# High and low activations side by side in one 512-column operand, and that form of matmul in 23 more steps

## The reference, cut to what matters

```python
u = jnp.einsum('bsd,de->bse', xn, w_in[l])
q, k, v, xr, gr, ga, gb = jnp.split(u, splits, axis=-1)
ya = chunked_band_attention(q, k, v, rel_table[l]) @ w_attn_out[l]
...
yb = (hr * jax.nn.gelu(gr)) @ w_rnn_out[l]
gates = jax.nn.sigmoid(jnp.concatenate([ga, gb], axis=-1) + b_merge[l])
g_a, g_b = jnp.split(gates, 2, axis=-1)
h = h + (g_a * ya + g_b * yb) @ w_o[l]
hn = rmsnorm(h, norm_ffn_g[l])
gu = hn @ w_ffn_in[l]
g, up = jnp.split(gu, 2, axis=-1)
h = h + (jax.nn.silu(g) * up) @ w_ffn_out[l]
```

## Time and profile before

| what | value |
|---|---|
| median of three runs | 1126.95 us |
| the profiled execution, its own time | 1127.41 us |
| its span in the trace | 1125.7 us |
| TensorE busy / weight loads busy | 1113.4 us / 1038.7 us |
| VectorE, ScalarE, GpSimd busy | 765.1, 589.9, 218.2 us |
| granted TensorE clock, mean | 0.997 of 2.4 GHz |
| HBM traffic | 166 GB/s over the span |

### The profile page before, as it was taken

One profiled execution on the slowest core, in us unless ns is written; L12 is line 12 of the kernel. 1 busy time (PEld: TensorE's weight loads), 2 busy tenths in 40 slices (PEclk: granted clock), 3 DMA queues, 4 the chain that ended last, 5 costly groups with the idle time before them and its releaser, 6 DMA issues.

```text
span 1125.7 us, 19980 instructions
## 1 busy us (share of the span) xinstructions
PE 1113.4 (99%) x7954; PEld 1038.7 (92%) x7954; DVE 765.1 (68%) x943; ACT 589.9 (52%) x791; POOL 218.2 (19%) x216
## 2 busy tenths in 40 slices
PE   8999999999999999999999999999999999999997
PEld 8999999999888889999999988888899999888887
DVE  6656984666877754599886777764467657876443
ACT  6546557545655543665664556643354445665332
POOL 2996002302000000167844010000030002000000
PEclk9999999999999999999999999999999999999999
DMA  9674442655655555446410356555545444656541
GB/s 299 204 236 150 150 132 96 225 185 169 206 187 186 186 188 190 146 148 188 152 39 2 112 161 197 193 196 186 187 150 188 151 144 148 200 189 215 189 149 38
DMA packets 154994, 187.31 MB, mean 166 GB/s; under 512 B 6544, under 2 KB 143920, under 8 KB 154928
## 3 DMA queue, kind: packets, MB, share of 16 engines
q1 hardware_dynamic: 151360, 184.06, 50.4%
q10 hardware_dynamic: 3568, 2.31, 0.7%
HBM read 185.29 MB, written 1.07 MB: 166 GB/s over the span
## 4 chain that ended last, share of the span: by engine, by line
PE 87%; POOL 5%; DVE 5%; issue 1%; ACT 1%; DMA 0%; DVEq 0%; POOLq 0%; ACTq 0%
PE PS L445 18%; PE PS L493 12%; PE PS L386 10%; PE PS L387 9%; PE PS L388 9%; PE PS L447 9%; PE PS L495 6%; POOL XN L911 2%; DVE WL L382 2%; POOL TAP L909 2%; POOL XN L906 1%; PE PS L453 1%; PE PS L452 1%; PE PS L454 1%; PE PS L2013 1%; PE PS L2026 1%
## 5 line engine op out<-in xcount | busy, mean ns | idle before, releaser
L382 DVE TENSOR_TENSOR WL<-RAW,WH 128x2048 fp32r<-128x2048 f32 x170 | 399.1, 2349 | 213.0 <-ACT WH L373 212.9
L373 ACT ACTIVATE WH<-RAW 128x2048 fp32r<-128x2048 f32 x170 | 325.0, 1912 | 219.1 <-PE PS L495 121.1
L445 PE MATMUL PS<-XHL,WH 128*128 128x512 f32 x864 | 300.9, 395 | 0.0
L386 PE MATMUL PS<-XHL,WH 128*128 128x256 f32 x832 | 240.3, 289 | 3.0 <-DVE WL L333 1.8
L447 PE MATMUL PS<-XHL,WL 128*128 128x256 f32 x864 | 239.6, 277 | 0.0
L387 PE MATMUL PS<-XHL,WH 128*128 128x256 f32 x832 | 236.0, 284 | 0.0
L388 PE MATMUL PS<-XHL,WL 128*128 128x256 f32 x832 | 236.0, 284 | 0.0
L493 PE MATMUL PS<-HHL,WH 128*128 (+1 forms) x592 | 205.4, 394 | 0.0
L445 PEld LDWEIGHTS PS<-XHL,WH 128*128 128x128 f32 x864 | 162.1, 188 | 37.5
L386 PEld LDWEIGHTS PS<-XHL,WH 128*128 128x128 f32 x832 | 160.2, 193 | 6.4 <-issue 2.8
L495 PE MATMUL PS<-HHL,WL 128*128 (+1 forms) x592 | 164.0, 277 | 0.0
(11 more groups left out here) (310 smaller groups left out, 1669.4 us busy)
## 6 DMA issues: line engine op xcount, KB each, us to landing
RAW<-in_mlp_w_up SPq DMA_DIRECT2D x32, 1024.0 KB, 5.4
RAW<-in_mlp_w_down SPq DMA_DIRECT2D x32, 1024.0 KB, 5.0
RAW<-in_w_in SPq DMA_DIRECT2D x25, 1024.0 KB, 5.2
RAW<-in_w_ffn_in_pairs SPq DMA_DIRECT2D x22, 1024.0 KB, 5.1
RAW<-in_dn_w_in SPq DMA_DIRECT2D x16, 1024.0 KB, 5.9
RAW<-in_mb_w_in SPq DMA_DIRECT2D x12, 1024.0 KB, 5.2
RAW<-in_w_ffn_out SPq DMA_DIRECT2D x11, 1024.0 KB, 4.9
RAW<-in_w_attn_out SPq DMA_DIRECT2D x4, 1024.0 KB, 5.8
```

The source lines that it names most:

```text
L373: act.activation(WH[:, k], RAW[:, k], ACT.Copy).then_inc(hi_done, 1)
L382: dve.tensor_tensor(WL[:, k], RAW[:, k], WH[:, k].bitcast(F32), ALU.subtract).then_inc(lo_done, 1)
L386: pe.matmul(out, wh, xh, start=start, stop=False, skip_group_check=True)
L445: pe.matmul(out.rearrange("p (e t) -> p e t", e=2), h[:, k, part], XHL[:, :, k], start=(k == 0), stop=False, skip_group_check=True)
```

## The change

It does three things. (1) XHL, OH/OL, HHL and DOH/DOL are laid out with the high and low run of one block side by side ([8, 2, 256]), so the 512-column operand is one run of 512 numbers; this touches every wide matmul of the kernel. (2) The wide form is used in gab 4 to 7, ao, ro 0 to 2, wo, do and mo: 23 steps. Ro 3 stays narrow and only takes its banks from the table. (3) A table PAIRS gives the PSUM banks of these steps, and the halves are added by new work: ScalarE's `low_to` and VectorE's `add_to` in gab, ao and ro 0 to 2, a second addition to H on VectorE in wo, do and mo.

```diff
-    XHL = sb("XHL", [P, 2, KB, TOK], F32R, 80)
-    XH, XL = XHL[:, 0], XHL[:, 1]
+    XHL = sb("XHL", [P, KB, 2, TOK], F32R, 80)
+    XH, XL = XHL[:, :, 0], XHL[:, :, 1]
...
-    HHL = sb("HHL", [P, 2, 32, TOK], F32R, Z + 0)
-    HH, HL = HHL[:, 0], HHL[:, 1]
+    HHL = sb("HHL", [P, 32, 2, TOK], F32R, Z + 0)
+    HH, HL = HHL[:, :, 0], HHL[:, :, 1]
...
+        PAIRS = {"qk": (4, 6, 2, 4, 6, 2, 4, 6), "gab": (None, None, None, None, 3, 5, 0, 3), "ao": (5, 0, 2, 4),
+                 "ro": (6, 0, 4, 2), "wo": (6, 4, 2, 6), "do": (6, 4, 2, 6), "mo": (5, 2, 0, 6)}
...
-                pe.matmul(out.rearrange("p (e t) -> p e t", e=2), h[:, k, part], XHL[:, :, k], start=(k == 0), stop=False,
+                if not halves_:
+                    mm = product(pe, out[:, 0:TOK], h[:, k, part], l[:, k, part], both[:, k, 0], both[:, k, 1], k == 0, k == KB - 1)
+                    continue
+                pe.matmul(out, h[:, k, part], both[:, k].rearrange("p e t -> p (e t)"), start=(k == 0), stop=False,
                           skip_group_check=True)
...
+        def low_to(act, st, out):
+
+            act.wait_ge(mm_done, st.count())
+            act.activation(out, wide_sides(st)[1], ACT.Copy).then_inc(s_.part_out, 1)
+
+        def add_to(dve, st, out, n):
+
+            dve.wait_ge(s_.part_out, n)
+            return dve.tensor_tensor(out, out, wide_sides(st)[0], ALU.add)
...
                 merge_gate(2 * st.j - 8)
-                merge_gate(2 * st.j - 7)
+                if st.j < 7:
+                    merge_gate(2 * st.j - 7)
+                act.wait_ge(s_.scanned, 8)
+                low_to(act, st, GAB[:, 2 * st.j:2 * st.j + 2])
+            merge_gate(7)
...
-                read_out(st, GAB[:, 2 * st.j:2 * st.j + 2])
+                blk = slice(2 * st.j, 2 * st.j + 2)
+                ch(add_to(dve, st, GAB[:, blk], part_no("gab") + st.j - 3))
+                ch.wait(dve)
+                dve.tensor_tensor(GAB[:, blk], GAB[:, blk], by_rows(2), ALU.mult).then_inc(freed[st.slot], 1)
...
-                    dve.tensor_tensor(hb, hb, bank(st), ALU.add).then_inc(freed[st.slot], 1)
+                    ch(dve.tensor_tensor(hb, hb, wide_sides(st)[1], ALU.add))
+                    ch.wait(dve)
+                    dve.tensor_tensor(hb, hb, wide_sides(st)[0], ALU.add).then_inc(freed[st.slot], 1)
...
-            steps(pe, seg["ao"], lambda st: multiply(pe, st, OH, OL))
-            steps(pe, seg["ro"], lambda st: multiply(pe, st, XH, XL, (s_.y_done, 0) if st.j == 0 else None))
-            steps(pe, seg["wo"], lambda st: multiply(pe, st, OH, OL, (s_.ml_done, 0) if st.j == 0 else None))
+            steps(pe, seg["ao"], lambda st: multiply_wide(pe, st, both=OHL))
+            steps(pe, seg["ro"], lambda st: multiply_wide(pe, st, (s_.y_done, 0) if st.j == 0 else None, halves_=st.j < 3))
+            steps(pe, seg["wo"], lambda st: multiply_wide(pe, st, (s_.ml_done, 0) if st.j == 0 else None, both=OHL))
```

More of the change, by code:

```diff
@@ L267, in build @@
           amf_out yf_out ty_out zg_done vn0 vn0_out s_done s_out w_done w_out vn1 vn1_out o_done o_out osq osum ostat osd
[L268 removed]
+          orows gated uq_zero yy oo low_out outg part_out low_rows low_added hi_piece lo_piece sp_ready""".split()
         s = {n: sem(n) for n in names}
@@ L430, in wide_sides, with multiply_wide @@
             return both[:, :, 0], both[:, :, 1]
-        def multiply_wide(pe, st, pieces=None, between=None):
+        def multiply_wide(pe, st, pieces=None, between=None, both=XHL, beside=None, halves_=True):
             pe.wait_ge(lo_done, st.count())
@@ L438, in multiply_wide @@
             for n, (b, k) in enumerate(order_of(pieces)):
+                if n == 4 and beside:
+                    beside()
                 if n == KB and between:
@@ L444, in multiply_wide @@
                 part = slice(b * P, b * P + P)
-                pe.matmul(out.rearrange("p (e t) -> p e t", e=2), h[:, k, part], XHL[:, :, k], start=(k == 0), stop=False,
+                if not halves_:
+                    mm = product(pe, out[:, 0:TOK], h[:, k, part], l[:, k, part], both[:, k, 0], both[:, k, 1], k == 0, k == KB - 1)
+                    continue
+                pe.matmul(out, h[:, k, part], both[:, k].rearrange("p e t -> p (e t)"), start=(k == 0), stop=False,
                           skip_group_check=True)
-                mm = pe.matmul(out[:, TOK:512], l[:, k, part], XH[:, k], start=False, stop=(k == KB - 1),
+                mm = pe.matmul(out[:, TOK:512], l[:, k, part], both[:, k, 0], start=False, stop=(k == KB - 1),
                                skip_group_check=True)
@@ L491, in multiply_rows @@
                 else:
-                    xhl = HHL[:, :, at, :].rearrange("p e k t -> p e (k t)")
-                    pe.matmul(out.rearrange("p (e t) -> p e t", e=2), h[:, k, part], xhl, start=first and k == 0, stop=False,
+                    pe.matmul(out, h[:, k, part], xhl, start=first and k == 0, stop=False,
                               skip_group_check=True)
@@ L1059, in low_half, with part_no @@
             act.activation(two(SG[:, st.slot]), wide_sides(st)[1], ACT.Copy).then_inc(s_.low_out, 1)
+        def part_no(name):
+            return {'gab': 0, 'ao': 4, 'ro': 8}[name]
+        def low_to(act, st, out):
[4 more added lines that the diff above has]
+            return dve.tensor_tensor(out, out, wide_sides(st)[0], ALU.add)
         def add_halves(dve, st, earlier):
@@ L1169, in _ @@
                 act.activation(XH[:, 2 * p:2 * p + 2], XN[:, 2 * p:2 * p + 2], ACT.Copy).then_inc(s_.yh_done, 1)
+                low_to(act, st, MU[:, 2 * p:2 * p + 2])
             def mix_high(p):
@@ L1178, in _ @@
                     mix_high(st.j - 1)
+                if st.j < 3:
+                    act.wait_ge(freed[(seg["ao"].first + st.j) % SLOTS], (seg["ao"].first + st.j) // SLOTS + 1)
+                    low_to(act, st, MU[:, 2 * st.j:2 * st.j + 2])
             mix_high(3)
@@ L1526, in _ @@
                 dve.tensor_tensor(XL[:, blk], XN[:, blk], XH[:, blk].bitcast(F32), ALU.subtract).then_inc(s_.y_done, 1)
-                dve.wait_ge(mm_done, st.count())
+                ch(add_to(dve, st, MU[:, blk], part_no("ao") + j + 1))
                 dve.wait_ge(s_.gab_done, 8)
-                dve.tensor_tensor(MIX[:, 2 * j:2 * j + 2], bank(st), GAB[:, 2 * j:2 * j + 2], ALU.mult).then_inc(freed[st.slot], 1)
+                ch.wait(dve)
+                dve.tensor_tensor(MIX[:, blk], MU[:, blk], GAB[:, blk], ALU.mult).then_inc(freed[st.slot], 1)
             def mix_lo(p):
@@ L1540, in _ @@
                     mix_lo(st.j - 1)
-                dve.wait_ge(mm_done, st.count())
-                dve.tensor_tensor(MU[:, blk], bank(st), GAB[:, 8 + 2 * st.j:10 + 2 * st.j], ALU.mult).then_inc(freed[st.slot], 1)
+                if st.j < 3:
+                    ch(add_to(dve, st, MU[:, blk], part_no("ro") + st.j + 1))
+                    ch.wait(dve)
+                    sum_ = MU[:, blk]
+                else:
+                    dve.wait_ge(mm_done, st.count())
+                    sum_ = wide_sides(st)[0]
+                dve.tensor_tensor(MU[:, blk], sum_, GAB[:, 8 + 2 * st.j:10 + 2 * st.j], ALU.mult).then_inc(freed[st.slot], 1)
                 dve.wait_ge(freed[st.slot], st.base // SLOTS + 1)
@@ L2123, in _ @@
             head_sums(3)
-            steps(pe, seg["do"], lambda st: multiply(pe, st, DOH, DOL, None if st.j else (s_.yy, 0),
-                                                     beside=None if st.j else last_rows))
+            steps(pe, seg["do"], lambda st: multiply_wide(pe, st, None if st.j else (s_.yy, 0), both=DOHL,
+                                                          beside=None if st.j else last_rows))
             def mlp(layer):
@@ L2151, in _ @@
             attn_pv(pe, 11)
-            steps(pe, seg["mo"], lambda st: multiply(pe, st, OH, OL, None if st.j else (s_.ol_done, 8)))
+            steps(pe, seg["mo"], lambda st: multiply_wide(pe, st, None if st.j else (s_.ol_done, 8), both=OHL))
             mlp(1)
```

19 lines of the change are left out of this document (10 added, 9 removed).

## The result

| | before | after |
|---|---|---|
| median of six runs each | 1126.65 us (1126.29 to 1126.96) | 1130.96 us (1130.27 to 1131.77) |
| profiled execution, its own time and span | 1127.41, 1125.7 us | 1130.8, 1129.1 us |

The ratio is 1.0042, interval 1.0032 to 1.0052: the changed kernel is slower by 0.42%, 4.3 us, where 3.2 us of gain were forecast. It lies 4.7 us above the upper end of the range.

The account below looks back on a forecast made before the run. TensorE, busy 99% of the span, was taken as the bound: 4.6 us saved by the form, less 0.45 for gab 7 and 0.9 for norm waits, layout zero, net 3.2, giving 1123.8 us; range 1101 to 1126.3.

Parts of the forecast that it names:

- what bounds the kernel: Whole kernel: TensorE, busy 99% of the span, sets the time; a wide step takes 5.54 us, a narrow one 5.76.
- Forecast: Whole kernel: the profiled 1127.41 us becomes 1124.2, and the median 1126.95 - 3.2 = 1123.8 us.
- (b): Savings eaten: new wide steps cost 5.65 us (2.5 saved), two stalls twice as large (2.7 us); 1127.1 us, chance 0.07.
- The form's saving: In the 23 new wide steps: 19 save 0.22 us each and wo's 4 save 0.11 each, 4.6 us in all.
- The layout: In all 1824 wide products: the one-run operand saves zero; the far end was 0.015 us a product, 27 us.
- Rival (a): In all wide products: the one-run operand saves 5 to 15 ns each, 9 to 27 us; 1115 to 1097 us, chance 0.35.
- the 38 us: In 1824 wide products: the most the layout could be worth by a skill page's 325 ns a product against 346.
- Gab 7: At its start: the new 0.60 us ScalarE copy delays WL to 195.86, and TensorE stalls 0.45 us.
- The norm waits: Behind wo, do and mo: the extra addition to H makes TensorE wait 0.3 us for each norm sum, 0.9 in all.
- ScalarE's and VectorE's new work: In the new wide steps: PSUM reads of 0.60 and 0.69 us fit and are hidden, except at gab 7 and the norms.
- rival (c): In ro, or all 23 steps: reading the halves becomes the bound, 0.46 us a step; 1128.9 to 1134 us, chance 0.07.

Follow-up runs that it names:

- experiment 4: The kernel before, with H one VectorE operation later in each step of wo, do and mo, all matmuls unchanged: 1135.75 us, ratio 1.0080.
- experiment 8: The kernel before, with H one VectorE operation later in the steps of wo only: 1130.02 us, ratio 1.0030.
- experiment 3: The whole change, but the last step of wo, do and mo narrow, so that H is complete one addition earlier: 1124.61 us, ratio 0.9988 to the kernel before.
- experiment 7: The whole change with wo, do and mo left narrow, so 11 new wide steps and one addition to H: 1125.27 us, ratio 0.9992 to the kernel before.
- experiment 6: The whole change plus two unhindered float32 matmuls at the end of the third step of fi, u0 and u1: 1126.89 us, ratio 1.0010 to the kernel before.
- experiment 1: The kernel before with only the new layout, high and low runs side by side, all products in their old form: 1126.57 us, ratio 1.0000.
- experiment 12: The kernel of experiment 3 plus two unhindered float32 matmuls in the middle of gab 6: 1125.15 us, ratio 0.9992 to the kernel before.
- experiment 2: The kernel before with only the wide form in the 23 steps, high and low runs still apart: 1129.06 us, ratio 1.0025.

## Why the prediction was wrong

**The step that failed** stands in the prediction's part on what bounds the kernel: a whole wide step takes 5.54 us, and the 5.65 us of fi 0 was taken as the price of coming straight out of narrow steps. All of "Forecast" rests on it: that the 91 wide steps outside the 23 keep their 5.54 us. The 5.65 us was the slow one of two steady rhythms, which can hold for a whole loop. What the change saves with 23 x 16 fewer matmuls it loses because 56 steps of fi, fo, u0 and w0 went from 346.5 to 353.3 ns a product: 6.1 us by the traces, and 1.6 for the late norm sums. That a later H alone can do this is shown on the kernel before by experiments 4 (only the delay of H, +9 us) and 8 (the delay in one place, exactly one stretch slow). That it is what did it in the change rests on experiments 3 and 7 (no delay, all loops fast), and less firmly: both also bring back the narrow step ahead of each loop, no run has the wide last step without the delay, and the change's own u1, with the same wait of 0.31 us as fi, stayed fast. The traces of the thirteen full kernels have 39 loops (fi, u0, u1 in each), which I sort by the norm sum at their start and by the rhythm ahead of it:

| norm sum | rhythm ahead | loops | slow behind sum and transposes |
|---|---|---|---|
| not held up | slow | 17 | 0 |
| held up | slow | 15 | 14 |
| held up | fast | 7 | 2 |
| not held up | fast | 0 | |

So in these traces a loop is slow only where its sum was held up. The change's u0 is one of the 14, its fi one of the 2; since 5 of 7 such loops stayed fast, the held-up sum does not decide the rhythm there by itself. None of the rivals held this; (b) gave 5.65 us to the new steps alone.

**The form's saving** was right in kind. At the same rhythm a wide step costs 5.54 against 5.76 narrow; from mo 0 to the norm sum in u1 the trace takes 31.06 us after and 31.60 before, 0.54 less. The sum starts 0.82 us behind the last product after and 0.36 before, which hides 0.46 of the gain; and 0.16 of it is that the first 24 products of u1 are fast after and slow before. So 0.84 is left for the four steps of mo, forecast 0.88. In gab 5 to ro 2 the slow rhythm halves the saving (10 x 0.11 = 1.1 us lost), and wo gets 0.22 a step rather than 0.11, since here fast products follow narrow ones (in experiments 3 and 6 wo is slow): 11 x 0.22 + 4 x 0.22 - 1.1 - 0.35 of stall = 1.85, measured 1.73.

**The layout**: zero was forecast and zero was measured (experiment 1). Rival (a), with 0.35, is refuted: the distance 0.23 to 0.24 of the 512-column matmul did not fall with the one-run operand. The 325 ns a product that stand behind the 38 us beside it appear in no run here; the lowest mean is 346.5.

**Gab 7.** TensorE, ScalarE and VectorE around its start (a timeline of all engines; 0.58 us is the new copy, 2.28 the low part):

```profile
189.45 0.58 ACT L1076 ACTIVATE GAB<-PS 128x512 f32<-128x512 f32 x1
...
189.93 1.90 ACT L373 ACTIVATE WH<-RAW 128x2048 fp32r<-128x2048 f32 x1
...
192.12 2.28 DVE L382 TENSOR_TENSOR WL<-RAW,WH 128x2048 fp32r<-128x2048 f32 x1
...
193.85 0.40 PE L454 MATMUL PS<-XHL,WH 128*128 128x512 f32 x1
...
194.45 0.51 PE L454 MATMUL PS<-XHL,WH 128*128 128x512 f32 x1
```

WL ends at 194.40, and with the opening's 1.47 us the forecast of 195.86 becomes 194.39: that end was right to 0.01 us. The stall is there too: from the last product of gab 6 to the second of gab 7 the trace has 194.91 - 193.85 = 1.06 us, where two products at 353 ns take 0.71. So it costs 0.35 us of the 0.45 forecast (TensorE, slow in gab 5 and 6, came a little later to it).

**The norm waits** came where they were forecast, but at nearly twice the price, and with a consequence that the forecast did not have. TensorE's waits after:

```profile
PE PS L617 <- POOL XN L595: 1.5, 4, 0.7
```

Less the 0.7 us that the first layer's sum waited before too, 0.8 us of idle time in three waits (0.32, 0.15, 0.31), forecast 0.9. But by the distances between the products around them the three sums cost 0.59, 0.42 and 0.58 us more than before, 1.6 in all: the sum itself starts 0.46 us late in u1, not 0.31, and its four matmuls take 0.11 longer (0.71 us against 0.60). The slow steps around two of them cost 6.1 us on top.

**ScalarE's and VectorE's new work** is hidden, as forecast, but for gab 7 and the norms: no other new wait of TensorE shows, and rival (c) did not occur.

**Left open.** What in TensorE makes the two rhythms. Why a pair of float32 matmuls turns them in the middle of a step of fi, and neither at its end nor in gab 6. Why the same instructions ran in different rhythms in different profiles (experiments 6, 7 and 12), and, if the wide spreads of experiments 2, 3 and 6 mean this, from execution to execution, while the kernel before and the change held their times within 1.7 us but for one execution. Whether a loop that is entered fast would also turn slow with no sum held up: no kernel has that case. In fi of the change the turn itself came at the transposes of L636, 3.3 us behind the wait; in all three loops of experiment 4 the turn also comes at the transposes, with the eight products between sum and transposes fast, and in experiment 8 the products are slow straight behind the sum. That the wait sets the turn up is an inference from experiments 4 and 8, not seen in the trace. In the last stretch 0.4 us of the gain is lost behind TensorE's last matmuls: from the start of the last transposes to the end of the span it takes 6.44 us after (1122.66 to 1129.10) and 6.06 before (1119.64 to 1125.70), by a cause that was not looked for.
